# Prompt attention scores as three products of split parts, with the queries and keys stored split, and wider rotary products for the sampled tokens

## What is computed

```
s = (einsum('bqhd,bkhd->bhqk', qn, k_nope) + einsum('bqhr,bkr->bhqk', qp, k_pe)).astype(float32) * ATTN_SCALE
s = where(key_pos <= q_pos, s, finfo(float32).min)
p = softmax(s)                                     # prompt: the queries of 1024 tokens over their own keys
...
s_past = einsum('bthc,bkc->bhtk', q_lat, past_ckv) + einsum('bthr,bkr->bhtk', q_pe, past_kpe)   # sampled
```

## Time and profile before

| | |
|---|---|
| runs, median (range) | 2883.55 us (2880.69 to 2885.36) |
| the profiled execution, its own time | 2889.95 us |
| its span | 2888.1 us |
| mean granted TensorE clock | 0.984 of 2.4 GHz |
| PE busy | 2819.2 us (98%), 18888 matmul records |
| DVE, POOL, ACT busy | 1483.4 (51%), 1036.8 (36%), 744.9 us (26%) |
| DMA | 314.46 MB, mean 109 GB/s |

### The profile page before, as it was taken

The page is one execution under the profiler, slowest core; times in us unless marked ns, Lnnn a source line. Parts: engine busy times, 40 slices in busy tenths (PEclk is TensorE's granted clock), DMA queues, the critical chain, the costliest instruction groups (busy, mean ns, idle before and its releaser), DMA issues.

```text
span 2888.1 us, 45655 instructions
## 1 busy us (share of the span) xinstructions
PE 2819.2 (98%) x18888; PEld 2527.0 (87%) x18888; DVE 1483.4 (51%) x2044; ACT 744.9 (26%) x1173; POOL 1036.8 (36%) x611
## 2 busy tenths in 40 slices
PE   8999999999999999999999999999999999999998
PEld 7999999899999995555666699999999999999998
DVE  3535877775756655555343456776652222222226
ACT  2111212353545453555332421101120000000000
POOL 3443333343333323554211123446533333333331
PEclk9999999999999997999999999999999999999999
DMA  5263223574756545223334342354211111111111
GB/s 144 70 195 120 82 89 112 168 190 139 186 145 172 155 122 151 66 65 106 143 132 181 141 152 101 131 180 133 67 45 44 45 50 44 44 44 45 49 51 60
DMA packets 315965, 314.46 MB, mean 109 GB/s; under 512 B 32144, under 2 KB 273045, under 8 KB 313334
## 3 DMA queue, kind: packets, MB, share of 16 engines
q1 hardware_dynamic: 253592, 200.76, 24.5%
q10 hardware_dynamic: 58646, 73.90, 7.5%
q0 software_dynamic: 3584, 37.75, 3.4%
HBM read 234.15 MB, written 78.21 MB: 108 GB/s over the span
## 4 chain that ended last, share of the span: by engine, by line
PE 80%; DVE 12%; ACT 3%; issue 3%; DMA 1%; ACTq 0%; POOL 0%; SPq 0%; DVEq 0%; POOLq 0%
PE ps L995 41%; PE ps L1185 12%; PE ps L1319 4%; DVE cv L2293 3%; PE ps L1343 3%; PE ps L1477 2%; PE ps L1333 2%; PE ps L1453 2%; PE ps L1433 2%; DVE cv L2287 1%; PE ps L1218 1%; PE ps L1222 1%; PE ps L1211 1%; PE ps L1604 1%; DVE cv L2295 1%
## 5 line engine op out<-in xcount | busy, mean ns | idle before, releaser
L794 POOL TENSOR_TENSOR whi<-raw,cst 128x1024 fp32r<-128x1024 f32 x160 | 311.3, 1946 | 1103.3 <-PE ps L995 882.8
L796 POOL TENSOR_TENSOR wlo<-raw,whi 128x1024 fp32r<-128x1024 f32 x160 | 433.5, 2709 | 12.5
L995 PE MATMUL ps<-ahi,whi 128*128 128x352 f32 x1728 | 375.4, 325 | 2.6 <-DVE alo L2668 1.9
L995 PE MATMUL ps<-alo,whi 128*128 128x352 f32 x1728 | 375.8, 326 | 0.0
L995 PE MATMUL ps<-ahi,wlo 128*128 128x352 f32 x1728 | 371.3, 324 | 0.0
L995 PEld LDWEIGHTS ps<-ahi,whi 128*128 128x128 f32 x1728 | 294.4, 189 | 3.3 <-DVE alo L2668 2.5
L995 PEld LDWEIGHTS ps<-ahi,wlo 128*128 128x128 f32 x1728 | 296.5, 189 | 0.0
L995 PEld LDWEIGHTS ps<-alo,whi 128*128 128x128 f32 x1728 | 295.7, 189 | 0.0
L1185 PE MATMUL ps<-xhi,whi 128*128 128x352 f32 x768 | 255.9, 333 | 0.4 <-ACT xraw L1787 0.4
L1185 PE MATMUL ps<-xhi,wlo 128*128 128x352 f32 x768 | 247.8, 323 | 0.0
L1185 PE MATMUL ps<-xlo,whi 128*128 128x352 f32 x768 | 247.8, 323 | 0.0
(11 more groups left out here) (368 smaller groups left out, 5053.7 us busy)
## 6 DMA issues: line engine op xcount, KB each, us to landing
raw<-in_w_in SPq DMA_DIRECT2D x61, 512.0 KB, 5.1
s_a<-d_acum SPq DMA_DIRECT2D x32, 512.0 KB, 7.4
d_xbc<-so ACTq DMA_DIRECT2D x24, 528.0 KB, 2.7
gt<-d_g SPq DMA_DIRECT2D x24, 528.0 KB, 3.6
raw<-in_w_ffn_gate SPq DMA_DIRECT2D x22, 512.0 KB, 3.9
raw<-in_w_ffn_up SPq DMA_DIRECT2D x22, 512.0 KB, 3.8
raw<-in_w_ffn_down SPq DMA_DIRECT2D x22, 512.0 KB, 3.6
d_z<-zo ACTq DMA_DIRECT2D x16, 528.0 KB, 5.2
```

Of the source, the lines that this page charges most:

```text
L794: pool.tensor_tensor(whi[s][:, :], raw[:, u], ones[:, 0:1].broadcast_to([P, UNIT]), ALU.mult).then_inc(sem("unit_hi"), k["unit_hi"].adds(1))
L796: pool.tensor_tensor(wlo[s][:, :], raw[:, u], whi[s][:, :].bitcast(F32), ALU.subtract).then_inc(sem("unit_split"), k["unit_split"].adds(1))
L995: last = pe.matmul(ps[0:m, 3 * b + c, 0:width], w(j), x[:, j, at:at + width], start=i == 0, stop=i == n - 1)
```

## The change

Queries and prompt keys are cut into upper and lower parts where they are made, ahead of their stores, and lie in DRAM as two arrays each; a call of `scores` makes three fp32r matmuls for each 512 keys in place of one float32 one. For each pair of heads ACT makes the upper parts (plain from PSUM, rotary from SBUF) and DVE subtracts them to get the lower ones; the bank set 1 is freed by DVE's subtraction, no longer by ACT's copy, and in the key stage both bank sets are (`lower_keys`). The rotary key is finished and cut in steps behind pairs 0, 1 and 2. The four pairs of DRAM arrays double what is stored and what SP loads for the attention. The first pair's lower parts take the place of the buffers of the last dense weights, so their loads wait for unit_done 74 and stand ahead of the values' loads; the first call of `scores` waits for both parts. The sampled tokens' queries are summed again by DVE from both parts (two operations, ahead of `earlier_rows` of the last pair but one). In `key_scores` the 32 rotary products of 128 columns of a sequence become 8 of 512 columns, whose moving operand steps over every second of eight slices.

```diff
-    d_q = scratch("d_q", [HEADS, QH, TOK])
-    d_k = scratch("d_k", [HEADS, NOPE, SEQ])
+    d_q = [scratch(f"d_q{part}", [HEADS, QH, TOK]) for part in range(2)]
+    d_k = [scratch(f"d_k{part}", [HEADS, NOPE, SEQ]) for part in range(2)]
     d_v = scratch("d_v", [HEADS, P, SEQ // P * VH])
-    d_kr = scratch("d_kr", [ROPE, TOK])
+    d_kr = [scratch(f"d_kr{part}", [ROPE, SEQ]) for part in range(2)]
+    d_krs = scratch("d_krs", [ROPE, NS])
...
-        qb.append([qk(f"qb{pp}{h}", [QH, SEQ]) for h in range(2)])
-        kb.append([qk(f"kb{pp}{h}", [QH, SEQ]) for h in range(2)])
+        for part in range(2):
+            qb.append([qk(f"qb{pp}{part}{h}", [QH, SEQ], F32R) for h in range(2)])
+            kb.append([qk(f"kb{pp}{part}{h}", [QH, SEQ], F32R) for h in range(2)])
...
 
         one = lambda d, h: d[bass.ds(h, 1)].rearrange("a p n -> (a p) n")
 
-        def rotary_keys(pp, name):
+        def rotary_keys(pp, part, name):
             for h in range(2):
-                sp.dma_start(kb[pp][h][NOPE:QH, :], d_kr[:, 0:SEQ]).then_inc(sem(name), k[name].adds(16))
-
-        def queries_keys(pp, pair, name):
+                sp.dma_start(kb[2 * pp + part][h][NOPE:QH, :].bitcast(F32), d_kr[part]).then_inc(sem(name), k[name].adds(16))
+
+        def queries_keys(pp, part, pair, name):
             for h in range(2):
-                for dst, src in ((qb[pp][h][:, :], one(d_q, pair * 2 + h)[:, 0:SEQ]), (kb[pp][h][0:NOPE, :], one(d_k, pair * 2 + h))):
-                    sp.dma_start(dst, src).then_inc(sem(name), k[name].adds(16))
+                for dst, src in ((qb[2 * pp + part][h][:, :], one(d_q[part], pair * 2 + h)[:, 0:SEQ]),
+                                 (kb[2 * pp + part][h][0:NOPE, :], one(d_k[part], pair * 2 + h))):
+                    sp.dma_start(dst.bitcast(F32), src).then_inc(sem(name), k[name].adds(16))
 
         def head_values(pp, pair):
             for h in range(2):
                 sp.dma_start(vb[pp][h][:, :, :].rearrange("p a n -> p (a n)"), one(d_v, pair * 2 + h)).then_inc(sem(f"head_full{pp}"), k[f"head_full{pp}"].adds(16))
 
         sp.wait_ge(sem("unit_split"), 74)
-        rotary_keys(0, "kr_full")
-        queries_keys(0, 0, "kr_full")
+        rotary_keys(0, 0, "kr_full")
+        queries_keys(0, 0, 0, "kr_full")
         sp.wait_ge(sem("unit_done"), 74)
+        rotary_keys(0, 1, "kr_full")
+        queries_keys(0, 1, 0, "kr_full")
         head_values(0, 0)
-        rotary_keys(1, "head_full1")
-        queries_keys(1, 1, "head_full1")
+        for part in range(2):
+            rotary_keys(1, part, "head_full1")
+            queries_keys(1, part, 1, "head_full1")
         head_values(1, 1)
         sp.wait_ge(sem("ssm_over"), 1)
...
             q, h, b = 4 * G + 3 - i // 2, i % 2, i % 2
             if G == 0 and i == 0 and not first:
-                pe.wait_ge(sem(f"head_full{pp}"), k[f"head_full{pp}"].next(96))
+                pe.wait_ge(sem(f"head_full{pp}"), k[f"head_full{pp}"].next(160))
             first_bank = 2 * b + (i // 2 % 2 if G == 0 else 0)
             pe.wait_ge(sem(f"s_read{b}"), k[f"s_read{b}"].held() - (1 if G == 0 and i >= 2 else 0))
             length = (q + 1) * P
             for c in range(0, length, 512):
                 w = min(512, length - c)
-                pe.matmul(ps[:, first_bank + c // 512, 0:w], qb[pp][h][:, q * P:(q + 1) * P], kb[pp][h][:, c:c + w], start=True, stop=True)
+                for m, (x, y) in enumerate(((0, 0), (0, 1), (1, 0))):
...
         pe.wait_ge(sem("uk_ready"), k["uk_ready"].next(4))
+        pe.wait_ge(sem("queries_whole"), k["queries_whole"].next(2))
...
-                for r in range(4 if c == 0 else 0):
-                    for s in range(2):
-                        for bank in range(4):
-                            rows_ = slice(32 * bank, 32 * bank + 32)
-                            pe.matmul(half(bank, s)[:, r * P:(r + 1) * P], qcur[b][rows_, 2 + bank, :], kpt[rows_, 2 * r + s, :],
-                                      start=r == 0, stop=False, skip_group_check=True)
+                for s in range(2 if c == 0 else 0):
+                    for bank in range(4):
+                        rows_ = slice(32 * bank, 32 * bank + 32)
+                        pe.matmul(half(bank, s), qcur[b][rows_, 2 + bank, :], kpt[rows_, s:NPG // 4:2, :], start=True, stop=False,
+                                  skip_group_check=True)
...
+        def upper_query(to, src):
+            act.activation(to, src, ACT.Copy).then_inc(sem("q_hi"), k["q_hi"].adds(1))
+
         def query_pair(p):
             b = p % 2
             act.wait_ge(sem("unit_done"), k["unit_done"].next())
             act.wait_ge(sem(f"q_stored{b}"), k[f"q_stored{b}"].same())
-            act.activation(thirds(qh[b]), out3(1), ACT.Copy).then_inc(sem("out_free1"), k["out_free1"].adds(1))
+            upper_query(thirds(qh[b][:, :]), out3(1))
             k["out_free0"].n += 1
+            k["out_free1"].n += 1
             act.wait_ge(sem("q_turned"), k["q_turned"].next())
-            for h in range(2):
-                act.dma_start(d_q[2 * p + h, NOPE:QH], qr[b][ROPE * h:ROPE * h + ROPE]).then_inc(sem(f"q_stored{b}"), k[f"q_stored{b}"].adds(16))
+            upper_query(qrs[b][0:NOPE, :], rot[0:NOPE])
+            if p == 2:
+                act.wait_ge(sem("key_turned"), k["key_turned"].next())
+                upper_query(krs2[R0:R1, :], small[R0:R1, :])
             act.wait_ge(sem("out_free1"), k["out_free1"].same())
-            for h in range(2):
-                act.dma_start(d_q[2 * p + h, 0:NOPE], qh[b][NOPE * h:NOPE * h + NOPE]).then_inc(sem(f"q_stored{b}"), k[f"q_stored{b}"].adds(16))
+            for t, d in ((qh[b], d_q[0]), (ql[b], d_q[1])):
+                for h in range(2):
+                    act.dma_start(d[2 * p + h, 0:NOPE], t[NOPE * h:NOPE * h + NOPE, :].bitcast(F32)).then_inc(sem(f"q_stored{b}"), k[f"q_stored{b}"].adds(16))
+            act.wait_ge(sem("q_split"), k["q_split"].next())
+            for part in range(2):
+                for h in range(2):
+                    r = NOPE * part + ROPE * h
+                    act.dma_start(d_q[part][2 * p + h, NOPE:QH], qrs[b][r:r + ROPE, :].bitcast(F32)).then_inc(sem(f"q_stored{b}"), k[f"q_stored{b}"].adds(16))
+
+        def rotary_out():
+            act.wait_ge(sem("q_split"), k["q_split"].next())
+            act.dma_start(d_krs, small[R0:R1, SEQ:TOK]).then_inc(sem("stored"), k["stored"].adds(16))
+            for part, r in enumerate((R0, R1)):
+                act.dma_start(d_kr[part], krs2[r:r + ROPE, 0:SEQ].bitcast(F32)).then_inc(sem("stored"), k["stored"].adds(16))
...
                 act.wait_ge(sem("sub_done"), k["sub_done"].next())
                 act.wait_ge(sem(f"k_stored{b}"), k[f"k_stored{b}"].same())
                 src = ps[:, 3 * b:3 * b + 2, :].rearrange("p a n -> p (a n)")
-                act.activation(kvh[b], src, ACT.Copy).then_inc(sem(f"out_free{b}"), k[f"out_free{b}"].adds(1))
+                act.activation(kvh[b][:, 0:SEQ], src, ACT.Copy).then_inc(sem("k_hi"), k["k_hi"].adds(1))
+                k[f"out_free{b}"].n += 1
                 act.wait_ge(sem(f"out_free{b}"), k[f"out_free{b}"].same())
                 h = 4 * s + 2 * half
-                act.dma_start(d_k[h:h + 2].rearrange("a p n -> (a p) n"), kvh[b]).then_inc(sem(f"k_stored{b}"), k[f"k_stored{b}"].adds(16))
+                for t, d in ((kvh[b], d_k[0]), (klo[b], d_k[1])):
+                    act.dma_start(d[h:h + 2].rearrange("a p n -> (a p) n"), t[:, 0:SEQ].bitcast(F32)).then_inc(sem(f"k_stored{b}"), k[f"k_stored{b}"].adds(16))
...
             dve.wait_ge(sem("half_done"), p + 1)
-            dve.wait_ge(sem(f"q_stored{p % 2}"), k[f"q_stored{p % 2}"].held(64))
+            dve.wait_ge(sem(f"q_stored{p % 2}"), k[f"q_stored{p % 2}"].held(128))
             if p:
-                dve.wait_ge(sem("q_turned"), k["q_turned"].same())
-            if p == 1:
-                dve.wait_ge(sem("key_turned"), k["key_turned"].same())
+                dve.wait_ge(sem("q_split"), k["q_split"].same())
             dve.tensor_tensor(thirds(rot[0:NOPE]), ps[NOPE:P, 0:3, 0:CH], thirds(rope_t[NOPE:P, 1]), ALU.mult).then_inc(step.sem, step.adds(1))
             dve.tensor_tensor(thirds(to), ps[0:NOPE, 0:3, 0:CH], thirds(rope_t[0:NOPE, 0]), ALU.mult).then_inc(sem("out_free0"), 1)
             dve.wait_ge(step.sem, step.same())
             dve.wait_ge(sem("out_free0"), 3 + p + 1)
-            dve.tensor_tensor(to, to, rot[0:NOPE], ALU.add).then_inc(sem("q_turned"), k["q_turned"].adds(1))
-
-        def turn_key():
-
-            dve.wait_ge(sem("out_free1"), 3)
-            dve.wait_ge(sem("q_turned"), k["q_turned"].same())
-            dve.tensor_tensor(rot[R0:R1], small[R1:R2, :], rope_t[R1:R2, 1], ALU.mult).then_inc(step.sem, step.adds(1))
-            dve.tensor_tensor(small[R0:R1, :], small[R0:R1, :], rope_t[R0:R1, 0], ALU.mult).then_inc(step.sem, step.adds(1))
-            dve.wait_ge(step.sem, step.same())
```

(36 more changed lines are left out.)

61 lines of the change are left out of this document (37 added, 24 removed).

## The result

The changed kernel takes 2895.8 us (median of 7 runs, 2890.59 to 2903.36) against 2882.72 us for the kernel before on the same chip (7 runs, 2876.3 to 2889.13): a ratio of 1.0057, 95% interval 1.0045 to 1.0069. It is some 16 us slower by the ratio (13 by these two medians); the forecast was 21 us faster, in a range that ended at 2875. The profiled execution took 2894.71 us, 4.8 more than that of before, 2889.95, which is above all seven runs of its kernel. So the two traces side by side account for 4.8 us; the other 8 to 11 have no place in them.

The account below looks back on a forecast made before the run. PE was taken to bound the kernel, with 80% of the chain. Terms -17 - 5 + 5 + 0.3 + 0.6 + 2 + 2 - 9 = -21 made 2869 us profiled, 2862.5 against the median 2883.55; 8 in 10: 2847 to 2875.

Parts of the forecast that it names:

- The scores: Prompt attention: three fp32r products cheaper than one float32, net 2.45 us a pair, -17 us (-13 to -25) over seven stretches.
- DVE's two sums: Sampled queries summed again on DVE, bounded by its 512-column copies: +0.3 us.
- The query stage: Query stage: DVE's subtractions covered, ACT's four more stores and drift hidden by the bank sets: +0.6 us.
- The key stage: Start of the key stage: PE waits for bank set 0, freed late by DVE's `klo`: +2 us.
- My own sign of being wrong: The forecast would be wrong if, among other signs, the key stage lost over 6 us.
- The stores' own +2: Key stage: 4.2 MB more stores, 336 GB/s asked where 344 is full: +2 us, between no wait and 12.
- The opening: First pair's calls ahead of the seven stretches: cheaper scores -5 us, against later loads +5 us.
- The loads' +5: First call of `scores` waits for six more loads, 1.57 MB, on full DMA engines: +5 us (3 to 7).
- The gain of 5 in its calls: First pair's G=0 calls and its `later_rows`, partly at the lower clock, get cheaper scores: -5 us.
- The sampled part: Rotary scores about 1.0 us in each sequence, 1.8 less in long ones, last gather binding: -9 us (-5 to -11).
- weight loads that are not hidden: Rival for the scores: each chunk pays three loads and products in turn, about 2901 us; 5% chance.
- Rival 2: Stores bind: key stage pays +10 instead of +2, query stage's stores land late; 2872 us, 15% chance.

Follow-up runs that it names:

- three_stores: The changed kernel with queries laid out in DRAM so that ACT stores a pair by three DMAs of 128 rows, not eight; ratio 0.9997 to the kernel before.
- two_products: The changed kernel without each score's third product (lower queries by upper keys); ratio 1.0006 to the kernel before.

## Why the prediction was wrong

- **The scores.** The step was "take 0.72 against 0.91". It costs 0.81 against 0.97: the 0.23 us a product hold (1.50 for six products of 512 columns), but what a call pays ahead of its first product is 0.12, not 0.03 to 0.06. A pair's sixteen calls save 2.33 us, not 3.2. The 128-key call's 0.39 was forecast at 0.38. The chain of 4.97 held to 0.01, with 0.67 us turned into waiting against 0.55. So 1.70 a pair in place of 2.45, 12 us in seven stretches. Of these DVE's two sums take 1.3 ("+0.3": they last 2.3 us together), 3.4 us at the lower clock from 1407.7 on about 1.5, and the first of the seven gained only 1.4, which leaves the table's 8.8 but for rounding.
- **The query stage**, the step that failed most. I wrote that ACT's "pairs fill nearly their 9.8 us" and may drift by 0.4 a pair "which the bank sets hide". The price came from one row of two stores, 1.24 us; eight take 5.8 to 6.8 from the first issue to the end of the last. From the third pair on ACT needs 10.4 to 11.4 us for a pair, PE 8.7 and, with the key tiles, 9.8; ACT's copy comes 2.5 us behind PE at the fourth pair and 4 us at the last, and at the end of the stage nothing hides that. "+0.6" was 4.3: 1.5 ahead of the third pair, where PE waited for DVE's turn, as forecast but twice as long (1.2 us), and 2.8 in waits for `ql`. The step behind it was another 9.2 (three_stores: removing five issues a pair takes 6.3 of these back).
- **The key stage.** The wait that I forecast at 2 us for `klo` was a wait of 7.9 us one step earlier, for a copy on DVE that I had only counted as "copies of 1.0". I asked who waits for the subtractions and not who waits for what is queued behind them. PE waited for no `klo` at all. My own sign of being wrong, a key stage that loses over 6 us, came true. The stores' own +2 was 0: the window above has the DMA engines at a share of 0.99 and 340 GB/s, which is the 344 that I had scaled from the rows, and nobody waits. The 435 GB/s of the Trainium skill ("DMA: Bandwidth & Descriptors", Where 436 GB/s comes from) I took wrongly: the same section calls it the ceiling of SBUF's ports and puts transfers between HBM and SBUF, as these are, at about 358.
- **The opening.** The loads' +5 was 7.6, a little over its bounds of 3 to 7. The gain of 5 in its calls was on its way (4.0 us up to the mask that stands at 1119 in the kernel before), and then PE's wait of 5.4 us for ACT took it back, and the lower clock, which had ended at 1134.6 and came again at 1138.1 for 6.8 us, another 1.2. The step had no term for the stage's last store, which shares the DMA engines with the loads.
- **The sampled part.** Right: 1.04 us, six gains, the last gather binding; -10.6 up to the eighth scores and -9.4 with the gather's wait behind them, for -9.
- **What was missing altogether**: the loop's place in the code, 5.5 us in the profile, 3.5 to 6 by the runs, 600 us behind the last stage that the change touches.
- **The rivals.** Slower was given 4%, by way of weight loads that are not hidden; they are hidden here for 96 rows too, as products of 512 columns start 0.23 us apart. Rival 2, stores that bind in the query and key stages at 15%, was right in place and wrong in cause: it is the issuing of stores on ACT, not their bytes. It was priced at +10; with it the forecast was 2872.

## What to carry to other kernels

Price a queue by its fullest period (the turn in which it has most to do) and follow its drift to the end of the stage, where no double buffer is left; eight stores of an engine that also computes are a load like any other. When a change adds loads to a full stretch, look for the smallest transfer there that somebody waits for, here a store of 64 KB that took 26 us. And if PE gains or loses instructions anywhere ahead of a long loop, compare the instruction packets of the two pages before looking for a cause in the loop.

## What the runs showed of the hardware

- A loop of 110 KB of PE's code runs without instruction packets at one place of the program; at another it fetches nine of 16 KB in every pass, and PE waits 0.7 to 1.3 us at each return.
- A store whose DRAM side has an outer dimension of 2 ran at 52 GB/s on a share of 0.13; the same bytes over 128 rows took 0.34 us to issue and disturbed nobody.
- Fp32r matmuls over 96 rows, each with its own weight load, start 0.23, 0.18, 0.12 and 0.115 us apart for 512, 384, 256 and 128 columns; the first of a call takes 0.05 (128 columns) to 0.10 us more.
- Thinner work came with a lower clock: two_products has eight places of 3.4 us at the lower level where the changed kernel has at most one, 1.5 us each, which is about the 10 us that are missing of its 27.
